# Latent attention on one core: another order of a group's projections, scores, transposes and modulation rows

## What is computed

```python
def latent_attention(x, pos, w_in, q_a_gain, w_q_up, kv_a_gain, w_kv_up, q_gain, k_gain, w_out):
    ...
    q = (rmsnorm(c_q, q_a_gain) @ w_q_up).reshape(B, S, B_HEADS, B_QK)
    kv = (rmsnorm(c_kv, kv_a_gain) @ w_kv_up).reshape(B, S, B_HEADS, B_NOPE + B_VDIM)
    k_nope, v = kv[..., :B_NOPE], kv[..., B_NOPE:]
    k = jnp.concatenate([k_nope, jnp.broadcast_to(k_rope[:, :, None, :], (B, S, B_HEADS, B_ROPE))], axis=-1)
    q = rmsnorm(q, q_gain)
    k = rmsnorm(k, k_gain)
    q = jnp.concatenate([q[..., :B_NOPE], rope(q[..., B_NOPE:], pos)], axis=-1)
    k = jnp.concatenate([k[..., :B_NOPE], rope(k[..., B_NOPE:], pos)], axis=-1)
    o = _causal_attention(q, k, v)
    return o.reshape(B, S, B_HEADS * B_VDIM) @ w_out
```

## Time and profile before

| | |
|---|---|
| median of 3 runs | 2503.65 us (2498.86 to 2504.4) |
| the profiled execution | 2499.47 us, span 2498.2 us |
| mean granted TensorE clock | 0.961 of full speed |
| busy: PE, DVE, ACT, POOL | 93%, 49%, 39%, 20% of the span |
| the latent groups | 1010.68 to 1161.43 us of the span |

### The profile page before, as it was taken

One profiled execution on the slowest core, in us unless ns is written; L12 is line 12 of the kernel. 1 busy time (PEld: TensorE's weight loads), 2 busy tenths in 40 slices (PEclk: granted clock), 3 DMA queues, 4 the chain that ended last, 5 costly groups with the idle time before them and its releaser, 6 DMA issues.

```text
span 2498.2 us, 37765 instructions
## 1 busy us (share of the span) xinstructions
PE 2326.4 (93%) x16663; PEld 2120.0 (85%) x16663; DVE 1221.8 (49%) x1521; ACT 969.2 (39%) x1145; POOL 506.6 (20%) x453
## 2 busy tenths in 40 slices
PE   6999999989999999889999899979999989888998
PEld 6998899979999998557999877867888877657997
DVE  5645566646555543445655345362122264545444
ACT  3433344434343433334444244333222233534442
POOL 2112434302111211220221101012202210230220
PEclk9999999989999999789999999989999999999999
DMA  6555433445555555666554310113332322213551
GB/s 242 175 173 173 139 122 133 136 169 174 182 179 185 180 182 173 229 237 236 172 183 155 124 35 18 34 68 101 101 98 88 102 96 85 68 51 93 181 183 68
DMA packets 205245, 344.72 MB, mean 138 GB/s; under 512 B 8845, under 2 KB 69498, under 8 KB 205082
## 3 DMA queue, kind: packets, MB, share of 16 engines
q1 hardware_dynamic: 205082, 342.31, 41.0%
HBM read 341.24 MB, written 1.05 MB: 137 GB/s over the span
## 4 chain that ended last, share of the span: by engine, by line
PE 80%; DVE 9%; POOL 4%; ACT 4%; issue 2%; SPq 0%; DMA 0%; DVEq 0%; POOLq 0%; ACTq 0%
PE PS L466 77%; PE PS L475 3%; DVE WL L452 2%; ACT WH L439 1%; POOL small L1454 1%; DVE rstd L587 1%; DVE XL L634 1%; POOL TMP L1463 1%; DVE XL L1002 0%; DVE al L998 0%; POOL small L1452 0%; DVE TMP L1382 0%; POOL TMP L1464 0%; DVE TMP L1387 0%; DVE al L1371 0%
## 5 line engine op out<-in xcount | busy, mean ns | idle before, releaser
L452 DVE TENSOR_TENSOR WL<-raw,WH 128x2048 fp32r<-128x2048 f32 (+2 forms) x281 | 651.6, 2331 | 720.7 <-ACT WH L439 720.7
L466 PE MATMUL PS<-XH,WH 128*128 128x256 f32 (+1 forms) x2336 | 699.3, 299 | 40.3 <-issue 15.3
L466 PE MATMUL PS<-XL,WH 128*128 128x256 f32 (+1 forms) x2336 | 692.9, 297 | 0.0
L466 PE MATMUL PS<-XH,WL 128*128 128x256 f32 (+1 forms) x2336 | 692.6, 297 | 0.0
L439 ACT ACTIVATE WH<-raw 128x2048 fp32r<-128x2048 f32 (+2 forms) x281 | 518.8, 1858 | 361.6 <-PE PS L466 361.1
L466 PEld LDWEIGHTS PS<-XH,WH 128*128 128x128 f32 x2336 | 451.6, 193 | 56.6 <-issue 18.5
L466 PEld LDWEIGHTS PS<-XL,WH 128*128 128x128 f32 x2336 | 452.6, 194 | 10.1
L466 PEld LDWEIGHTS PS<-XH,WL 128*128 128x128 f32 x2336 | 452.2, 194 | 10.0
L466 PE MATMUL PS<-WH,XH 128*128 128x256 f32 (+2 forms) x944 | 287.3, 304 | 17.3 <-DVE XL L634 8.5
L466 PE MATMUL PS<-WL,XH 128*128 128x256 f32 (+2 forms) x944 | 279.1, 296 | 0.0
L466 PE MATMUL PS<-WH,XL 128*128 128x256 f32 (+2 forms) x944 | 278.9, 295 | 0.0
(11 more groups left out here) (232 smaller groups left out, 2573.2 us busy)
## 6 DMA issues: line engine op xcount, KB each, us to landing
raw<-in_ffn_w_in SPq DMA_DIRECT2D x88, 1024.0 KB, 5.1
raw<-in_w_mod SPq DMA_DIRECT2D x48, 1024.0 KB, 5.2
raw<-in_ffn_w_out SPq DMA_DIRECT2D x40, 1024.0 KB, 4.9
raw<-in_a_w_in SPq DMA_DIRECT2D x36, 1024.0 KB, 4.9
raw<-in_w_mlp_in SPq DMA_DIRECT2D x32, 1024.0 KB, 5.5
raw<-in_w_mlp_out SPq DMA_DIRECT2D x32, 1024.0 KB, 5.0
raw<-in_gla_w_in SPq DMA_DIRECT2D x12, 1024.0 KB, 5.0
raw<-in_attn_w_qkv SPq DMA_DIRECT2D x6, 1024.0 KB, 5.0
```

Of the source, the lines that this page charges most:

```text
L452: dve.e.tensor_tensor(self.WL[j % NRAW][:, 0:nk * nn], self.raw[j % NRAW][:, 0:nk * nn], wh.bitcast(F32), ALU.subtract).then_inc(*self.lo. ...
L466: return self.pe.e.matmul(out, l, r, start=start, stop=stop, skip_group_check=skip)
```

## The change

The same instructions are issued in another order on TensorE, ScalarE, VectorE and GpSimd. On TensorE the scores of heads 0 and 1 stand between the q and the k/v projection; the first modulation row stands behind the V products of head 1; a second one stands behind those of head 2 and the third at the end. The rows are transposed into bank 4 (bank 2 in the last group) instead of bank 2. On ScalarE the exponentials of heads 0 and 1 stand ahead of k's squares, and a row is copied out only when the next row is begun or at the pass's end. On VectorE, scores 0 and 1 stand ahead of q's scaling, and this and the cosine product ahead of k's sums; the sine products are added later (`rotated`). On GpSimd q's sine products stand ahead of k's power.

```diff
-    LAT_FILLS = ((1, 3, 5), (0, 2, 4))
+    LAT_FILLS = ((0, 4), (0, 2))
...
+            fill = lambda: self.pe_mods.send(self.LAT_FILLS[not more])
             if more:
                 up(w_qu[:, (hs + 1) * 384:(hs + 2) * 384], 0, 3, 384, 0, ("lat", "q", hs + 1))
                 self.empties([0, 1], (self.emptied, ("lat", "q", hs + 1)))
+            if own:
+                score(hs, 0)
+                score(hs, 1)
+            if more:
                 up(w_kvu[:, (hs + 1) * 512:(hs + 2) * 512], 3, 2, 512, 2, ("lat", "kv", hs + 1))
                 self.empties([2, 3], (self.emptied, ("lat", "k", hs + 1)), (self.evac, ("lat", "v", hs + 1)))
...
+            else:
+                fill()
+            if own:
+                turn_p(hs, 0)
+                score(hs, 2)
+                turn_p(hs, 1)
+                pv(hs, 0)
+                score(hs, 3)
+                pv(hs, 1)
+            fill()
+            if more:
+                turn(hs + 1, 0)
+            if own:
+                turn_p(hs, 2)
+                pv(hs, 2)
+            if more:
+                fill()
+            if own:
+                turn_p(hs, 3)
+            if more:
+                turn(hs + 1, 1)
+            else:
+                fill()
+            if own:
+                pv(hs, 3)
+            if more:
+                fill()
...
             if more:
                 self.act_begin()
                 queries(hs + 1)
+            if own:
+                score(hs, 0)
+                score(hs, 1)
+            if more:
                 self.act_begin()
                 keys(hs + 1)
...
+            else:
+                self.fill_act(0)
+            if own:
+                score(hs, 2)
+                score(hs, 3)
+            self.fill_act(0)
+            if more:
+                turn(hs + 1, 0)
+            self.fill_act(0)
+            if more:
+                turn(hs + 1, 1)
+                self.fill_act(0)
             self.act_settle()
...
             if more:
                 self.dve_begin()
                 sums(0, hs + 1)
+            if own:
+                score(hs, 0)
+                score(hs, 1)
+            if more:
+                scaled(0, hs + 1)
                 self.dve_begin()
                 sums(1, hs + 1)
...
+            if own:
+                turn_p(hs, 0)
+                score(hs, 2)
+            if more:
+                rotated(0, hs + 1)
+                scaled(1, hs + 1)
+            if own:
+                turn_p(hs, 1)
+                score(hs, 3)
+            if more:
+                rotated(1, hs + 1)
+            fill()
+            if own:
+                turn_p(hs, 2)
+            if more:
+                fill()
+            if own:
+                turn_p(hs, 3)
+            fill()
...
             for w in range(2):
                 head_norm(w, hs)
-            for w in range(2):
                 rotate(w, hs)
```

More of the change, by code:

```diff
@@ L1563, in latent_pe @@
         for hs in range(-1, 4):
-            more = hs < 3
+            more, own = hs < 3, hs >= 0
+            fill = lambda: self.pe_mods.send(self.LAT_FILLS[not more])
             if more:
@@ L1707, in rotate @@
             C = self.tB[w][0]
-            x, q = XR[w], QR[w]
             dve.wait_ge(self.emptied, ("lat", ("q", "k")[w], hs))
@@ L1713, in rotate, with rotated @@
                 dve.wait_ge(self.turned, ("lat", w, hs - 1, 1))
-            dve.e.tensor_tensor(q, x, C.unsqueeze(2).to_broadcast([128, 2, 4, 96]), ALU.mult).then_inc(*self.v_step.up(("lat", "cos", w, hs)))
+            dve.e.tensor_tensor(QR[w], XR[w], C.unsqueeze(2).to_broadcast([128, 2, 4, 96]), ALU.mult).then_inc(*self.v_step.up(("lat", "cos", w, hs)))
+        def rotated(w, hs):
+            q = QR[w][:, :, :, 64:96]
             dve.wait_ge(self.v_step, ("lat", "cos", w, hs))
             dve.wait_ge(self.p_step, ("lat", "sin", w, hs))
-            dve.e.tensor_tensor(q[:, :, :, 64:96], q[:, :, :, 64:96], T2[w], ALU.add).then_inc(*self.rotated.up(("lat", w, hs)))
+            dve.e.tensor_tensor(q, q, T2[w], ALU.add).then_inc(*self.rotated.up(("lat", w, hs)))
         def sums(w, hs):
@@ L1767, in latent_dve @@
         for hs in range(-1, 4):
-            more = hs < 3
+            more, own = hs < 3, hs >= 0
+            fill = lambda: self.dve_mods.send(self.LAT_FILLS[not more][1])
             if more:
```

## The result

| | |
|---|---|
| the change, median of 18 runs | 2521.39 us (2501.84 to 2542.93) |
| before, median of 18 runs beside them | 2498.86 us (2495.84 to 2504.52) |
| ratio, 95% interval | 1.0075 (1.0062 to 1.0089) |
| profiled execution of the change | 2542.93 us, span 2541.6, clock 0.941 |
| a second profiled execution of it | 2522.97 us, span 2521.7, clock 0.950 |

The change made the kernel 22.5 us slower by the medians. The ratio leaves out the three slowest of its 18 runs (2541.01 to 2542.93 us, over 1.5% above its fastest, the first profiled execution among them); the median of the other 15 is 2518.75 us, 19.9 above before. Its runs spread over 41 us, those of before over 8.7. The first profiled execution is the slowest of the 18, so I read the second one, 1.6 us above the median, as the main profile of the change, and the first beside it.

A forecast was written before the change was run, and what follows sets the result against it. TensorE, busy in 93% of the span, was taken as the bound, moved only by its waits and clock. Terms 12 + 5 + 2 = +19 on 2499.5 gave 2518.5, plus half of 4.2: 2521 us, range 2503 to 2536.

The forecast's parts named there:

- The stop for the exponentials: In a group, TensorE's 2.41 us wait for head 0's exponentials would go, covered by the k/v projection.
- The two new stops: Before the V products of heads 0 and 1, TensorE would wait 1.65 and 2.5 us for VectorE's copy.
- The smaller ones: Waits of 0.75 and about 0.9 us beside later rows, 1.4 each ahead of group 0, about 1.8 in the last group.
- The clock: In groups 0 to 2, it would fall to half behind the two new waits and last through the first row.
- Two thirds of the way: The point taken between two ends for half clock in groups 0 to 2: +4 us in each group.
- end (ii): In groups 0 to 2, half clock stays to the group's end: group 40.1 us, +6.0.
- end (i): In groups 0 to 2, full clock returns after the first row and q's transposes: group 34.3 us, no gain.
- Groups 0 to 2 together: Three groups, each slower by 4 us through half clock: +12 us.
- Ahead of group 0: The stretch there would pay for late row copies on ScalarE and longer half clock: +5 us (3.5 to 6).
- Last group: Its second row waits for ScalarE's late copy of the first: +2 us, ends 0 and +4.
- The clock holds: Rival, 13%: full clock stays in groups 0 to 2, three groups at 30.3 us, total 2497 us.
- A late transfer: Rival, 5%: a transfer becomes late, costing 1 to 3 us for each of six blocks: 2525 to 2537 us.

The follow-up runs named there:

- e1_busy: The changed kernel with head 1's transposes issued five times and head 3's scores four times in groups 0 to 2, filling its stops: 2499.93 us, 1.0007 to before.
- e2_copies: The changed kernel with VectorE's order alone altered, copies of transposed heads 0, 1 and 2 moved earlier: 2487.18 us, ratio 0.9949 to before.
- e5_both: The changed kernel with both repairs, VectorE's earlier head copies and ScalarE's row copies right behind each row's products: 2472.76 us, ratio 0.9889 to before.
- e10_both_bank2: The kernel with both repairs, but the first row transposed into bank 2 as before the change: 2500.32 us, ratio 1.0001 to before.
- e3_rowcopy: The changed kernel with ScalarE's order alone altered, each modulation row copied out of PSUM right behind its products: 2494.4 us, ratio 0.9993 to before.
- e9_before_busy2: The kernel before with both stops filled in groups 0 to 2, by repeated head 1 scores and first half row products: 2492.55 us, ratio 0.9971.
- e4_before_busy: The kernel before with head 1's scores issued four times in groups 0 to 2, filling its 2.41 us stop: 2498.1 us, ratio 0.9998.
- e6_row_early: The changed kernel with the first row of groups 0 to 2 put back behind head 0's transposes: 2500.97 us, ratio 1.0012 to before.
- e11_both_pool: The kernel with both repairs, but GpSimd in the order before the change, powers of q and k first: 2476.03 us, ratio 0.9906 to before.

## Why the prediction was right

The forecast was 2521 in a range of 2503 to 2536, slower with 75%; the median is 2521.39. The mechanism was the one foreseen, but that the number fits to 0.4 us is luck. The forecast was 19.4 us above a base of 2501.6, which is half of the three runs' surplus over the profiled execution; the 18 runs of before have a median of 2498.86, so the base was 2.7 us too high. The rise was 22.5 us and not 19.4: 17.9 in the groups of the second execution, and the rest mostly behind them, of which the forecast knew nothing. Step by step:

**The stop for the exponentials** went, as said.

**The two new stops** were put at 1.65 and 2.5 us, released by VectorE's copy; they measure 1.64 to 1.65 and 1.94 to 2.62 over the six groups of the two executions. The prediction puts 3.0 us of wall time between them; by its own terms it is 1.34 (10.6 to 11.95), and it measures 1.59. The smaller ones: 0.65 ahead of head 2's V products (0.75 said), up to 0.64 ahead of the third row (0.9 said), 1.26 twice ahead of group 0 (1.4 said), 1.91 in the last group (1.8 said). Counting each engine's queue by durations from one profile gave these waits to within 0.3 us where TensorE ran at full clock; where it was slow, it came later and waited less (2.27, 1.94 and 0.21).

**The clock** fell behind the pair of stops and stayed through the first row in each group that was seen. "Two thirds of the way" between 34.3 and 40.1 gave 38; of the six groups in the two executions three are 39.1 to 39.9, near end (ii), and one is 34.7, which is end (i). Group 0 (37.4 and 37.7) is a third kind: the clock returned in it as in end (i), but its q projection still ran at half clock from the stretch ahead, 2.7 us that the forecast didn't have. So the two thirds are an average of unlike groups, and which group gets which end was not foreseen. e1_busy, e2_copies and e5_both show the cause: take the stops away or fill them and the clock is 0.89 to 1.00.

**The terms.** Groups 0 to 2 together: +12 said, 111.98 against 101.35 of before (150.75 less 27.94 and 21.46) is +10.6 in the second execution, +15.4 in the first. Ahead of group 0: +5 said, +5.3 and +3.7. Last group: +2 said, +1.9 and +4.9; the first of these executions exceeds my end of +4 because its half clock lasted there. The sum of +19 stands beside 17.9 and 24.0.

**What was mis-sized or not seen.** The edits that I judged one by one hang together through the clock. Bank 4 had a credit of 1.2 us and is worth 27.6 once the copies are on time (e10_both_bank2). The row copy had about 3 us of direct waits ahead of group 0 and 2 in the last group, and its repair alone is worth 27 by medians (e3_rowcopy), 16 of them seen in the stage. The repairs of 34 and 27 us give 48.6 together and not 61; a likely reason, not shown by itself, is that each also takes half clock from where the other acts. And I gave no thought to the spread of 41 us between runs of the change. It goes with the clock: the mean granted clock is 0.962 in its fastest run and 0.941 in the three slowest.

**The rivals.** "The clock holds" at 2497 was the other side, by way of a pair of stops that doesn't bring it down. It falls: in each of the six groups profiled the clock went to half there. With its condition made true by filling the stops it gives 2499.93, with added work in it. "A late transfer" did not show: the DMA share went down in the groups (0.55 to 0.68) and up to 0.87 in e5_both, and the one stop of 0.8 us for weights in the change is in the kernel before too.

## What to carry to other kernels

Where TensorE is busy over 90% of the span and still at half clock for stretches, count the stops of 1 to 3 us and not the busy time, and give the engine that ends them (here VectorE's copy of 0.56 us) the small, awaited operation ahead of the large ones that nobody waits for yet. An order of TensorE's work can be judged only with the other engines' orders fitted to it: the same order was 22.5 us slower than before or, with the two repairs, 26.6 us faster. Filling a stop with repeated matmuls is a cheap experiment that prices the stop before the repair is written. It needs more than one run and more than one profile: where the clock falls and rises, equal stops cost unequal time.

## What the runs showed of the hardware

Added work made kernels faster: 21.5 us against the change in e1_busy, 0.3% against before in e9_before_busy2.

Single stops of 2.15 us (e4_before_busy) and 2.47 us (e10_both_bank2), behind work at full speed, were followed by 1.2 GHz. Shorter ones were followed by it in some groups and not in others of one execution: the stop of 1.73 us in e6_row_early in groups 0 and 1 and not in group 2, the stop of 1.17 us in e11_both_pool in group 2 and not in groups 0 and 1. Some 3 us of half clock also stand behind stops of no more than 0.81 us (group 1 of e9_before_busy2, group 2 of e1_busy). No length of a single stop seen here decides alone. The Trainium skill (TensorE: Matmul & The Clock Gate, Part 1) gives as its rule for the fall an idle stretch longer than any of these, and beside it a kernel in which frequent short idles were enough; the traces disagree with the rule, and no run here shows which short idles it takes.

The way back also differs: in the same kernel group 2 took 34.67 us in one execution and 39.11 in the other, from equal stops (1.65 and 2.6). The four runs of the kernel that keeps full clock in the groups lie within 2 us (e5_both); versions that don't spread by 41 (the change, 18 runs) and 14 (e3_rowcopy, 12 runs).
